# A transformer block pair on one core: two modulation slabs before the first projection, a bias table laid out by the host, and a condition row asked for earlier

## What is computed

```python
def first_block(x, c, positions, w_ada, b_ada, g_norm1, w_in, g_na_q, g_na_k, na_rpb, ...):
    mod = jax.nn.silu(c) @ w_ada[l] + b_ada[l]
    shift1, scale1, gate1, shift2, scale2, gate2 = jnp.split(mod[:, None, :], 6, axis=-1)
    h = rms_norm(x, g_norm1[l]) * (1.0 + scale1) + shift1
    proj = h @ w_in[l]
    na_q, na_k, na_v, q_lat, kv_lat, k_rot, gate_na, gate_mla = jnp.split(proj, split_at, axis=-1)
    qa = rms_norm(na_q.reshape(B, S, NA_HEADS, NA_HEAD_DIM), g_na_q[l])
    ka = rms_norm(na_k.reshape(B, S, NA_HEADS, NA_HEAD_DIM), g_na_k[l])
    y_na = neighbourhood_attention(qa, ka, va, na_rpb[l])      # scores + bias from na_rpb
    ...
    h2 = rms_norm(x, g_norm2[l]) * (1.0 + scale2) + shift2
    return x + gate2 * moe_ffn(h2, ...)
```

## Time and profile before

| | us |
|---|---|
| median of 3 runs | 1055.96 (1055.14 to 1057.81) |
| the profiled execution's own time | 1057.58 |
| its span, first to last instruction | 1055.8 |
| TensorE busy in the span | 1012.4 (96%) |
| chain of work that ended last | TensorE 85%, DMA 8%, VectorE 4% |

### The profile page before, as it was taken

One profiled execution on the slowest core, in us unless ns is written; L12 is line 12 of the kernel. 1 busy time (PEld: TensorE's weight loads), 2 busy tenths in 40 slices (PEclk: granted clock), 3 DMA queues, 4 the chain that ended last, 5 costly groups with the idle time before them and its releaser, 6 DMA issues.

```text
span 1055.8 us, 16485 instructions
## 1 busy us (share of the span) xinstructions
PE 1012.4 (96%) x6434; PEld 711.7 (67%) x6434; DVE 455.2 (43%) x1112; ACT 282.6 (27%) x656; POOL 160.6 (15%) x154
## 2 busy tenths in 40 slices
PE   6998999999989999999899999999989999999998
PEld 4775868788647556555356655665449998998577
DVE  1376998686621321212112122222335652657941
ACT  3224365302511111212111211113322111213951
POOL 0000030215000000000000000001015963391001
PEclk9999999999999999999899999999999999999999
DMA  9999997469999999999999999999998434320001
GB/s 386 336 421 421 422 410 316 169 239 354 366 387 421 396 421 420 422 418 421 421 421 421 405 420 421 421 420 420 421 416 316 159 123 157 119 82 1 1 2 41
DMA packets 50463, 336.59 MB, mean 319 GB/s; under 512 B 5776, under 2 KB 8464, under 8 KB 10832
## 3 DMA queue, kind: packets, MB, share of 16 engines
q1 hardware_dynamic: 46976, 329.01, 76.8%
q10 hardware_dynamic: 3024, 4.79, 1.6%
q0 software_dynamic: 384, 1.70, 0.4%
HBM read 334.43 MB, written 1.05 MB: 318 GB/s over the span
## 4 chain that ended last, share of the span: by engine, by line
PE 85%; DMA 8%; DVE 4%; issue 1%; ACT 1%; SPq 0%; DVEq 0%; ACTq 0%
PE bank L1343 15%; PE bank L1452 11%; PE bank L1388 7%; PE bank L1242 5%; DMA ring<-experts 5%; PE bank L1108 4%; PE bank L1132 3%; PE bank L697 3%; PE bank L1175 3%; PE bank L1550 3%; PE bank L991 3%; PE bank L1603 2%; DMA ring<-stream 2%; PE bank L838 2%; PE bank L764 2%; PE bank L1008 2%
## 5 line engine op out<-in xcount | busy, mean ns | idle before, releaser
L1343 PE MATMUL bank<-ring,arena 128*32 128x512 f32 (+1 forms) x1112 | 176.8, 605 | 10.4 <-DMA ring<-experts 10.4
L1343 PEld LDWEIGHTS bank<-ring,arena 128*32 128x32 f32 (+1 forms) x1112 | 51.4, 121 | 115.8 <-issue 115.7
L1739 POOL TENSOR_TENSOR hT<-hT 128x256 f32<-128x256 f32 x30 | 28.5, 951 | 611.9 <-ACT hT L1820 610.2
L1388 PE MATMUL bank<-ring,conds 128*32 128x512 f32 (+1 forms) x560 | 88.8, 596 | 6.9 <-DMA ring<-experts 3.1
L2790 DVE TENSOR_TENSOR yhalf<-bank,yhalf 128x512 fp32r<-128x512 f32 x48 | 33.2, 692 | 82.2 <-ACT yhalf L2077 82.2
L2773 DVE SCALAR_TENSOR_TENSOR conds<-bank,gcol,conds 128x256 f32<-128x256 f32 x24 | 11.6, 484 | 125.2 <-ACT conds L2067 111.0
L2013 ACT ACTIVATE arena<-bank,mod 128x256 f32<-128x256 f32 x96 | 40.4, 472 | 78.1 <-PE bank L1108 77.9
L1388 PEld LDWEIGHTS bank<-ring,conds 128*32 128x32 f32 (+1 forms) x560 | 25.8, 119 | 52.0 <-issue 46.2
L1108 PE MATMUL bank<-picked,halves 128*128 128x256 f32 x384 | 57.8, 294 | 0.5 <-ACT arena L2013 0.5
L1108 PEld LDWEIGHTS bank<-picked,halves 128*128 128x128 f32 x384 | 49.0, 189 | 10.2 <-issue 9.1
L2498 DVE SCALAR_TENSOR_TENSOR resid<-bank,mod,resid 128x256 f32<-128x256 f32 x40 | 18.8, 482 | 77.7 <-PE bank L1175 25.4
(11 more groups left out here) (487 smaller groups left out, 1827.1 us busy)
## 6 DMA issues: line engine op xcount, KB each, us to landing
ring<-experts SPq DMA_DIRECT2D x187, 1024.0 KB, 13.4
ring<-stream SPq DMA_DIRECT2D x118, 1024.0 KB, 12.7
ring<-experts SPq DMA_DIRECT2D x8, 512.0 KB, 9.0
resid<-x SPq DMA_DIRECT2D x1, 1024.0 KB, 5.0
arena<-c_rows ACTq DMA_DIRECT2D x2, 512.0 KB, 12.3
resid<-ctx ACTq DMA_DIRECT2D x1, 1024.0 KB, 9.0
keys_room<-experts SPq DMA_DIRECT2D x1, 1024.0 KB, 10.4
arena<-stream SPq DMA_DIRECT2D x1, 1024.0 KB, 13.4
```

The lines of the kernel that those rows point to most:

```text
L1343: mm = mmul(o[at:at + n_slots, :], xg_of(m, kk)[:, at:at + n_slots], w[g][:, k, :], start=(kk == 0), stop=(kk == KT - 1))
L1388: mm = mmul(o[at:at + n_slots, :], aT[:, f, at:at + n_slots], w[g][:, 2 * c + f, :], start=(f == 0), stop=(f == 1))
```

## The change

1. **Order on TensorE and in the ring.** The second batch (ada1 1 and ada1 5) now stands ahead of `two_ks(0, 0)`; its fold stays behind it. Since slabs are asked for in program order, in 0 and in 1 come fifth and sixth in the ring, ada1 1 and ada1 5 third and fourth.
2. **Position bias.** The host lays the table out as each partition needs it (7,008 B in one piece); one DMA takes the place of two, and the waits on `bias_in` count 48 instead of 64.
3. **Condition row.** ScalarE issues the DMA of `c_row` one batch earlier, after the third batch's copy and so ahead of `cs`, `rq` and `ve`. Its Silu comes after the results of in 1 (s == 1) and not after those of in 0; VectorE's wait for it moves from before the first sum to after the second, just ahead of the first weighing.

```diff
             ada_fold(("first", 0))
-            two_ks(0, 0)
             ada_slab("ada1", 1)
             ada_slab("ada1", 5)
+            two_ks(0, 0)
             ada_fold(("first", 1))
...
-            pool.wait_ge(S("bias_in"), 64)
+            pool.wait_ge(S("bias_in"), 48)
...
                 ada_quarters(("first", i))
+                if i == 2:
+                    act.dma_start(c_row, crow_d.rearrange("p (a b) -> p a b", a=4)).then_inc(S("vec_in"), 16)
                 if i == 3:
                     act.dma_start(cs[:, C_EARLY:C_W], consts_d[:, C_EARLY:C_W]).then_inc(S("const_in"), 16)
                     act.dma_start(rq[:, 0:2].bitcast(I32), pos_d).then_inc(S("const_in"), 16)
                     act.dma_start(ve[:, V_EARLY:V_W], vecs_d[:, V_EARLY:V_W]).then_inc(S("const_in"), 16)
-                    act.dma_start(c_row, crow_d.rearrange("p (a b) -> p a b", a=4)).then_inc(S("vec_in"), 16)
...
-            for r in range(2):
-                src = bass.AP(rpb_d.tensor, (5 - r) * 31 - 48, [[1, 64], [15 * 31, 8], [1, RUN]])
-                act.dma_start(braw[64 * r:64 * r + 64, :, :], src).then_inc(S("bias_in"), 16)
+            act.dma_start(braw, rpb_d).then_inc(S("bias_in"), 16)
...
-                if s == 0:
+                if s == 1:
                     act.wait_ge(S("vec_in"), 32)
                     a.activation(c_row, c_row, ACT.Silu).then_inc(S("silu_c"), 1)
-            act.wait_ge(S("bias_in"), 64)
+            act.wait_ge(S("bias_in"), 48)
...
-            dve.wait_ge(S("silu_c"), 2)
             for j in range(8):
                 dve.wait_ge(S("sq_qk"), j + 1)
                 at = 16 * (j % 2) + 4 * (j // 2)
                 v.tensor_reduce(heads[:, at:at + 4], ...).then_inc(S("heads_summed"), 1)
+                if j == 1:
+                    dve.wait_ge(S("silu_c"), 2)
                 for i in ((), (0, 1), (), (2,), (), (3,), (), (4, 5))[j]:
                     weigh_slab(i)
...
+    bias = np.ascontiguousarray(x["na_rpb"][0][:, :, ::-1]).reshape(-1)
+    rpb = bias[(5 - np.arange(2))[:, None, None, None] * 31 - 48 + np.arange(64)[None, :, None, None] + ...].reshape(P, 8, RUN)
...
-        rpb=x["na_rpb"][0][:, :, ::-1],
+        rpb=rpb,
```

More of the change, by code:

```diff
@@ L3177 @@
     experts = np.concatenate([gu, dn], 1)
+    bias = np.ascontiguousarray(x["na_rpb"][0][:, :, ::-1]).reshape(-1)
+    rpb = bias[(5 - np.arange(2))[:, None, None, None] * 31 - 48 + np.arange(64)[None, :, None, None] + 15 * 31 * np.arange(8)[None, None, :, None]
+               + np.arange(RUN)[None, None, None, :]].reshape(P, 8, RUN)
     consts, consts2 = shape_constants()
```

## The result

The changed kernel takes 1065.16 us (median of 6 runs, 1063.99 to 1065.45), the kernel before 1055.69: the medians lie 9.5 us apart (0.90%). The ratio given with the result is 1.0074 with a 95% interval of 1.0061 to 1.0087, which is 7.8 us (6.4 to 9.2). The medians' 9.5 us lie just above that interval. By either figure the change is slower; 4.2 us were forecast. The time lies 2 us above the top of the range. The profiled execution took 1065.45 us with a span of 1063.6.

A forecast was written before the change was run, and what follows sets the result against it. TensorE, busy 96%, was taken as the bound, neck and neck with slabs from 48.85 us. Terms -2.5 (order), -3.0 (slab waits), 0 (bias), +8.2 (gates), +1.5 (clock) gave +4.2, so 1060.2 us; range 1052.0 to 1063.2.

The forecast's parts named there:

- c_row's price: ScalarE's queue: c_row's 32 packets an engine alternate with slab packets, 11.5 us, plus 2.5 fixed; about 14 us issue to landing.
- The order: TensorE's start: ada1 1 and ada1 5 fill idle time at full clock, 2.5 us gained; in 3 starts at 46.4.
- Slabs: SyncE's slab loads from in 4 to in 7 no longer late; those waits going give 3.0 us, nothing more.
- the signs: Things the new profile should show, among them SyncE's long wait on in 0 gone and CAST at 50 to 54.
- The second rival: SyncE's queue still runs dry, constants land at 47 to 48.5, total 1054 to 1057 us; chance 0.18.
- The bias: Position bias DMA in one piece: 2.1 us of DMA time, off the path; bounds 0 and 2.1, taken 0.
- C: Time at which the constants (cs, rq, ve) land: taken as 51.7 us, range 50.5 to 53.2, against 41.9 before.
- The first rival: DMA engines pass a run of small packets in one turn; faster, 1050.5 to 1052.6 us; chance 0.20.
- The chain: VectorE and ScalarE work after the constants land: frees bank 2 4.0 us later and bank 1 16.9 us later.
- The clock: TensorE at its lower clock after the idle time before in 5: 1.5 us, bounds 0 and 3.0.
- The sum: All terms added at in 7's start: 84.1 against 79.92, so +4.2 us for the kernel, 1060.2 us.
- the forecast's case: Late constants make TensorE wait for banks; 1060.2 us, spanning 1057.5 to 1063.2; chance 0.62.

## Why the prediction was wrong, and where it was right

The sign and the mechanism came true. The steps that failed are two terms of the sum: c_row's price, whose fixed part was taken as 2.5 us and was 5.6, so that the constants landed 2.3 us later than worked out; and the price of the lower clock, taken as 1.5 us and 3.0 on the path.

**The order: right.** in 3 was to start at 46.4 and started at 46.62; the clock from 18 to 20 us was to be 1.00 and was. The first pair of ada1 records had no idle time before it, but stood at 16.31 and not at 15.3: this execution's first matmuls took longer (the fold before it stands 1.1 us later than in the earlier trace rows). That cost little, because in 0's slab (0.28 us of idle time at 18.52) ended last.

**Slabs: right in effect, wrong in one sign.** Their waits are gone and no slab was late. SyncE's wait on in 0 is not gone, as the signs said it would be; it became harmless. The working itself had in 0 read to the end only at 40.3 (40.8 measured), so the wait was in it. The second rival, a queue that runs dry, did not happen: 421 GB/s from 43 to 47 us.

**The bias: right in the sum, wrong as a part.** Alone it gives the 2.1 us at in 7 that were its upper bound. In the change I had put it at nothing, since slabs no longer bind; without it the change takes 1.05% more, 11 us. The working had counted its bytes and not its packets, nor who stands in the issue behind them. The sum did not suffer, because it was made for the bias in one piece.

**c_row's price: mis-sized, 2.2 us.** The step put the constants at C = 51.7; they landed at 53.96. What stood behind c_row was right to a tenth: by issue and landing time `cs` landed 3.9 us behind c_row, `rq` 2.6 and `ve` 2.8 behind each other (3.9, 2.6, 2.7 worked out). All of the miss is in c_row's 16.2 us for 14.0. 386 packets in 8 us are 24 an engine, 0.33 us a turn (0.36 worked out), so 32 turns take 10.6; the fixed part is then 5.6 us and not 2.5. I had taken x's 2.5, from a queue that was empty, over ctx's 4.0, from a queue beside full slabs, which was the nearer case; even that was too low. In the first part of it nothing moves: no packet of q10 stands in the stretch from 31 to 32 us, although the issue was at 28.50. The trace of the kernel before had a nearer case that the working did not use: SyncE issues a slab at 43.00, beside the pieces of the bias, and no packet of it moves before 48 us.

```profile
q1 hardware_dynamic: 52, 0.42, 100.0%
```

**The first rival: refuted, twice.** 387 against 386 packets, and 7.9 against 16.2 us for the same bytes. The rule that the rival took from the Trainium skill, "DMA: Bandwidth & Descriptors", section "Queues, rings and completion order" (a whole packet of some 9 to 17 descriptors from one ring before the next), does not agree with these counts, if a row of the profile's count is a descriptor.

**The chain: right in its order, 0.5 us short.** Bank 2 was free C + 4.0 after the constants, as worked out (57.97). Bank 1 came C + 17.4 after them and not C + 16.9. Slab 2 took 0.9 us more than worked out, and the other steps 0.4 less. Its two passes took 1.75 and 1.69 us, those of slabs 0 and 1 1.28. What ran beside them was GpSimd with its adds of the bias:

```profile
66.26 4.56 POOL L1725 TENSOR_TENSOR bias_room<-bias_room,cs 128x256 f32<-128x256 f32 x4 [64.56 <-DMA arena<-c_rows]
```

In the kernel before the four adds took 2.60 us at 55.92, where VectorE ran no pass. That both are slowed fits what the Trainium skill says, "SBUF — State Buffer", section "Who interferes with whom": an instruction of VectorE with two inputs from the on-chip memory contends with one of GpSimd that reads there. These passes and adds show the size, about a third on one side and three quarters on the other. The run with the order alone has the adds later (74.77 to 80.45): there slab 2's passes take 1.28 us, and three passes of slabs 4 and 5, which run beside the adds, take 1.69 to 1.70.

**The clock: mis-sized, 1.3 us on the path.** The prediction took 1.5 us, the price of eight records, once. Both restarts paid nearly 3: 9.93 and 10.04 us for 7.07, with a granted clock of 0.50 (the lower level, 1.2 GHz) in the stretches 57 to 62 and 71 to 76 us. The first of these costs nothing, since in 5 waits for bank 1 behind in 4 in any case; the second is on the path. The bound of 3.0 held it, the value taken did not: eight records end within 3.5 us, so their row could show no more than the lower clock did in that time. The working also said that the engine had mostly stood idle before that fall of the clock; the earlier trace rows show idle times of 0.58 and 1.67 us there and no more, and with the second of them filled the clock stayed at 1.00.

**The sum.** in 7 was put at 84.1 and started at 88.19: 2.3 (constants), 0.5 (chain) and 1.3 (clock). The span grew by 7.8 and the profiled time by 7.9, which is what the ratio says (7.8), so by the ratio the miss is 3.6 us and these three terms cover it. The medians grew by 9.5: the profiled execution of before lay 1.9 us above the median of its runs and that of the changed kernel 0.3 above its own. That last 1.6 us is a difference between executions that no row explains. "A microsecond at in 7 is one of the whole kernel" held, by the ratios, to within 2.7 us in all kernels of the table; that is as much as several of them differ by.

**The range.** Its top, 1063.2, was the forecast's case with its latest constants (53.2). With 54.0 and 3 us of clock it would have been about 1064.0, with the chain's half microsecond 1064.5. The sign, the place (banks held by ScalarE's copies, not slabs) and the mechanism were right; the size, 4.2 us for 7.8 to 9.5, was about half.

## What to carry to other kernels

Before closing a hole in the busiest DMA queue, look for what lands in that hole from another queue. Here a transfer of n packets an engine beside a queue of 8-KB packets paid n turns, each with one of the neighbour's packets (a third of a microsecond where its own were small), and a fixed part that was longer than at the start of the kernel (5.6 us for 2.5). Give such transfers few long packets (4 KB for 1 KB halved c_row's time), or put them in line in the queue that is full. And where a wait moves, keep long work that nobody waits for (here the weighing) behind short work that frees a bank.

## What the runs showed of the hardware that I had not expected

- An engine that issues a DMA can stand in the issuing instruction: 16.4 us for two issues on ScalarE in the run with the order alone, 15.1 in the run without the bias in one piece, 7.7 us for c_row's on SyncE. ScalarE came back when an earlier transfer of its queue had landed (c_row at 60.7, the vectors at 54.2), with the pieces of the bias still to come; what sets the limit is not shown. ScalarE computes nothing meanwhile.
- A restart of TensorE behind idle time took 1.7 to 3.0 us more for 32 records. The idle times were 3.5 to 14.6 us, and the price did not grow with them (3.0 behind 3.5 and behind 14.6; 1.7 behind 9.5, when c_row's DMA was back behind the constants).
- Beside full-sized slabs the fixed part of a transfer in the second queue was 5.6 us, of which 3.8 to 4.0 passed before its first packet (issue at 28.50, first packets between 32.25 and 32.50).
